# An mLSTM cell on one core: C0 and v as the stationary side of the samples' numerators, and the prompt's sums of weights first

## What is computed

```python
w = jnp.exp(dlog - m_t[..., None])
s_inter = jnp.exp(inter - m_t)
qk = jnp.einsum('bthd,bshd->bhts', qc, kc) * w
num = s_inter[..., None] * jnp.einsum('bthd,bhde->bhte', qc, cm) + jnp.einsum('bhts,bshe->bhte', qk, vc)
den = s_inter * jnp.einsum('bthd,bhd->bht', qc, nv) + jnp.sum(qk, axis=-1)
h = num / jnp.maximum(jnp.abs(den), jnp.exp(-m_t))[..., None]
...
c_new = dec[..., None, None] * cm + jnp.einsum('bshd,bshe->bhde', kw, vc)
```

## Time and profile before

| | us |
|---|---|
| median of three runs | 2201.51 |
| the profiled execution | 2201.16 |
| its span in the profile | 2199.4 |
| TensorE matmul busy | 2156.8 |
| VectorE busy | 1244.7 |
| GpSimd busy | 1203.1 |
| ScalarE busy | 423.2 |

### The profile page before, as it was taken

How to read it: one execution, slowest core, us unless ns; L and a number is a source line. 1 busy time by engine, 2 the same in 40 slices (tenths; PEclk the granted TensorE clock), 3 DMA queues, 4 the chain that set the end, 5 groups by cost and what they waited for, 6 DMA issues and landing times. The chain is left out here.

```text
span 2199.4 us, 38981 instructions
## 1 busy us (share of the span) xinstructions
PE 2156.8 (98%) x15839; PEld 2019.4 (92%) x15839; DVE 1244.7 (57%) x2095; ACT 423.2 (19%) x780; POOL 1203.1 (55%) x1228
## 2 busy tenths in 40 slices
PE   9989899999999999999999999999999999999998
PEld 9988789989999999999999995587699999999997
DVE  6888875454625344676557645772754364435263
ACT  6224541222000000121202113421422220000002
POOL 7675666526656655666657650032254365665663
PEclk9999999999999999999999999999999999999999
DMA  6224344212222222224433323552332122222221
GB/s 219 77 87 145 112 144 192 78 39 78 77 95 78 77 82 89 76 92 153 152 145 136 142 100 141 203 192 78 120 137 75 39 79 95 77 79 94 77 78 62
DMA packets 41809, 235.95 MB, mean 107 GB/s; under 512 B 4672, under 2 KB 10048, under 8 KB 16584
## 3 DMA queue, kind: packets, MB, share of 16 engines
q1 hardware_dynamic: 24512, 157.57, 20.2%
q10 hardware_dynamic: 17160, 76.38, 9.1%
HBM read 200.05 MB, written 33.89 MB: 106 GB/s over the span
## 5 line engine op out<-in xcount | busy, mean ns | idle before, releaser
L501 POOL TENSOR_TENSOR wlo<-raw,whi 128x512 fp32r<-128x512 f32 (+1 forms) x684 | 827.4, 1219 | 112.6 <-ACT whi L1253 69.9
L494 POOL TENSOR_SCALAR whi<-raw 128x512 fp32r<-128x512 f32 x512 | 365.3, 714 | 824.1 <-PE psum L596 771.3
L596 PE MATMUL psum<-xnh,whi 128*128 128x288 f32 (+1 forms) x2784 | 607.6, 296 | 13.2 <-DVEq L210 3.6
L596 PE MATMUL psum<-xnh,wlo 128*128 128x288 f32 (+1 forms) x2784 | 603.9, 295 | 0.0
L596 PE MATMUL psum<-xnl,whi 128*128 128x288 f32 (+1 forms) x2784 | 603.8, 295 | 0.0
L596 PEld LDWEIGHTS psum<-xnh,whi 128*128 128x128 f32 x2784 | 451.9, 189 | 20.4 <-issue 11.8
L596 PEld LDWEIGHTS psum<-xnh,wlo 128*128 128x128 f32 x2784 | 451.8, 189 | 0.0
L596 PEld LDWEIGHTS psum<-xnl,whi 128*128 128x128 f32 x2784 | 451.8, 189 | 0.0
L596 PE MATMUL psum<-hh,whi 128*128 128x288 f32 x992 | 212.0, 295 | 2.1 <-DVE hl L2330 2.1
L596 PE MATMUL psum<-hl,whi 128*128 128x288 f32 x992 | 211.8, 294 | 0.0
L596 PE MATMUL psum<-hh,wlo 128*128 128x288 f32 x992 | 210.7, 293 | 0.0
(11 more groups left out here) (459 smaller groups left out, 2766.1 us busy)
## 6 DMA issues: line engine op xcount, KB each, us to landing
raw<-in_w SPq DMA_DIRECT2D x145, 1024.0 KB, 4.8
C<-in_C ACTq DMA_DIRECT2D x4, 1024.0 KB, 4.8
o_cp<-mvt ACTq DMA_DIRECT2D x4, 1024.0 KB, 3.9
o_cs<-C ACTq DMA_DIRECT2D x4, 1024.0 KB, 6.5
t_xc<-xc ACTq DMA_DIRECT2D x3, 1152.0 KB, 7.3
t_z<-mv ACTq DMA_DIRECT2D x3, 1152.0 KB, 4.1
t_q<-mq ACTq DMA_DIRECT2D x3, 1152.0 KB, 4.2
t_k<-mk ACTq DMA_DIRECT2D x3, 1152.0 KB, 4.2
```

What stands on the lines that cost most here:

```text
L494: pool.tensor_scalar(whi[:, s, c], raw[:, s, c], 1.0, 1.0, ALU.mult, ALU.mult).then_inc(S("slab_hi"), 1)
L501: ins = pool.tensor_tensor(wlo[:, s, c], raw[:, s, c], whi[:, s, c].bitcast(F32), ALU.subtract)
L596: ins = pe.matmul(bank(g, 2 * m + b)[:, 0:t1 - t0], W[wi][:, kk, m0 + m, :], r[:, kk, t0:t1], start=(at_first and wi == 0 and r is rh), st ...
```

## The change

In the group `den` the order becomes: the prompt's sums of weights (four products, which need only `wt`), the sample's sums with `n0b` (after the wait for `cell_qs`), the sample's sums with `ones` (after `cell_smp`), and last, after the wait for C0 (`cell_c`), the sample's numerators. These are now made feature-major at once: for each of the four blocks of 128 features, four products with a 128x128 block of C0 as stationary side and `qs` (64 columns) moving, and one with a 64x128 block of `vt5` stationary and `wts` (64 columns) moving, all added up in the same 64 columns of bank 3. The five 512-column products, ScalarE's copy of their result, the four transposes and the two signals between them are gone. The thresholds of the two semaphores at the end of the cell are renumbered.

```diff
                 pe.wait_ge(S("cell_pt"), n + 1)
-                pe.wait_ge(S("cell_qs"), n + 1)
-                pe.wait_ge(S("cell_smp"), n + 1)
-                pe.wait_ge(S("cell_c"), 16 * (n + 1))
-                for d in range(ML_T):
-                    mm(B[2][0:TS, :], qs[:, d, :], C0[:, d, :], d == 0, False)
-                mm(B[2][0:TS, :], wts[:], vt5[:], False, True).then_inc(S("bank_filled"), 1)
                 for j in range(NTB):
                     mm(B[0][:, P * j:TP], ones[:], wt[:, blk(j):blk(j) + TP - P * j], j == 0, j == NTB - 1)
+                pe.wait_ge(S("cell_qs"), n + 1)
                 for d in range(ML_T):
                     mm(B[1][:, 0:TS], n0b[:, d, :], qs[:, d, :], d == 0, False)
+                pe.wait_ge(S("cell_smp"), n + 1)
                 mm(B[1][:, 0:TS], ones[0:TS, :], wts[:], False, True)
-                pe.wait_ge(S("bank_read"), n + 1)
+                pe.wait_ge(S("cell_c"), 16 * (n + 1))
                 for e in range(ML_T):
-                    ins = pe.transpose(B[3][:, TS * e:TS * e + TS], tm[0:TS, 1, P * e:P * e + P], ident[0:TS, 0:TS])
+                    out = B[3][:, TS * e:TS * e + TS]
+                    for d in range(ML_T):
+                        mm(out, C0[:, d, P * e:P * e + P], qs[:, d, :], d == 0, False)
+                    ins = mm(out, vt5[:, P * e:P * e + P], wts[:], False, True)
                 group_close(ins, g)
...
-            pe.wait_ge(S("bank_read"), ML_H + 1)
+            pe.wait_ge(S("bank_read"), 1)
...
-                act.wait_ge(S("bank_filled"), ML_H + 1)
+                act.wait_ge(S("bank_filled"), 1)
...
-                act.wait_ge(S("bank_filled"), n + 1)
-                act.activation(tm[0:TS, 1, 0:ML_DH], bank(GR["cell", h, "den"], 2)[0:TS, :], ACT.Copy).then_inc(S("bank_read"), 1)
```

## The result

The changed kernel takes 2215.49 us (median of six runs) against 2203.07 us of six runs of the kernel before beside it. The ratio is 1.0062, with a 95% interval of 1.0052 to 1.0072: 11 to 16 us slower, where I had forecast no difference that can be told. The profiled execution has a span of 2215.2 us against 2199.4. The page of the changed kernel, the lines that answer to the earlier trace rows, does not show why at this grain: TensorE is busy for as large a share as before.

What follows compares the result with a forecast made beforehand. TensorE, busy 98% of the span at a granted clock of nine tenths or more, bounds the kernel. Heads' 0.35 + 0 + 0.46 + 0.46 = +1.27 us on 2201.16 gave 2202.4, stated as 2202.6; range 2198.6 to 2205.0.

Steps and rivals of the forecast that it cites:

- The start of `den`: `den` no longer waits first for C0, so it opens earlier: -0.44 us in the first head, -0.22 in the others.
- The products: In `den`, 4.90 us per head removed, four blocks of 1.40 us (5.60) added; net +0.79 first head, +0.68 others.
- a sign of being wrong: The prediction called itself wrong if `den` is under 8.0 or over 10 us.
- The price of a change of shape: In `den`, a weight load switching between 128 and 64 rows costs 0.15 us more than one staying in shape.
- Rival (a): Changes of shape in `den` cost nothing: -2.6 us, 2198.6; chance 13%.
- rival (c): In `den`, each record waits for its predecessor's sum in PSUM: 0.27 us a record, +27 us, 2228; chance 6%.
- rival (b): `den` starts no earlier, since freeing the PSUM half is as late as C0: +2.3 us, 2203.5; chance 15%.
- ScalarE: Its 0.59 us copy goes, its first-head sums start some 4 us earlier; worth nothing for TensorE.
- the forecast's 1.27: Predicted net slowdown over four heads, in us: 0.35 + 0 + 0.46 + 0.46.
- The 0.49 us at `kv`: Second head's `kv` already stands 0.49 us for ScalarE's last read of `den`, so that head's +0.46 counts 0.
- Slower by over 0.2%: Whole kernel slower by more than 4.4 us, from records waiting on PSUM and a little of a no-earlier `den` start; 8%.

Runs made afterwards that it cites:

- rows_128: The changed kernel with `vt5` and `wts` filled up with rows of zeros, so `den` has no change of shape; 0.9993 of the kernel before, 1.5 us below.
- double_columns: The changed kernel with `qs` and `wts` moved twice, 128 columns, the copy into unused columns of bank 3; 1.0014 of the kernel before, 3.1 us above.
- swap_only: The kernel before with the operand swap alone, in the old order, blocks first in `den`; 1.0051 of the kernel before, 11 us above.
- cols_48: rows_128 with 48 of the 64 sample columns moved in the C0 and v products; 1.0016 of the kernel before, 3.5 us above.
- cols_32: rows_128 with 32 of the 64 sample columns moved in the C0 and v products; 1.0035 of the kernel before, 7.7 us above.
- v_pairs: The changed kernel with two blocks' C0 products, then their two v products, and again: 6 changes of shape per head, not 10; 1.0033 of the kernel before.
- run 64: Not a run or kernel: the words come from "it had run 64-column products", where TensorE executed products with 64 moving columns.
- change_again: The changed kernel itself run once more, beside cols_48 and cols_32 on the same chip; 1.0075 of the kernel before, 16.5 us above.

## Why the prediction was wrong

**The start of `den`: right in place, a bit small.** From `kT` to `den` are 2.69 us in the first head of the changed kernel, 3.32 before: -0.63, where I took -0.44 with a bound of -0.62. The bracket of the row names VectorE's signal now, as the step said it would. In the second head 1389.54 - 1387.73 = 1.81 against 2.03: -0.22, as forecast.

**The products: right at the full clock, and only there.** Block 1.40 us, `den` 9.14 us in the first head, both as computed. In the second head `den` is 11.06 us, over the 10 us that the prediction itself named as a sign of being wrong. The price of a change of shape, 0.15 us from two rows, is 0.14 by rows_128. Rival (a), that it costs nothing, is out; rival (c), that each record waits for its predecessor, is out too (0.11 a record); rival (b) is out, since `den` starts earlier in both heads above.

**ScalarE: right.** In the changed kernel its sums start at 1337.65 in the first head instead of 1342.29, and nobody gains by it.

**The failed step** is one that the prediction did not even count as a step. It read the page's clock row, nine tenths or more in every slice, as a constant of the kernel, took every duration at 2.4 GHz, and summed them for a stretch that the kernel before doesn't have: 1344.90 - 1338.02 = 6.9 us in which TensorE does nothing but 64-column products bound by their loads. That a row of nines is no proof of one level could be seen in the kernel before. Its last slice reads nine like the others, and this is the view of its last 7.5 us, in which TensorE has no work left and the granted clock is 0.50:

```profile
2191.90:2199.40 7.50, 0.00 (x0) 0.00 (x0) 2.30 (x5) 1.25 (x3) 2.29 (x3) 0.50 0.45 157
```

Rows 5 seemed to be the proof that such a run keeps its pace, but that run is half as long, and has no change of shape in it. rows_128 and double_columns show that each of the two by itself would have been harmless (a run of 64-column products without a change of shape; the ten changes of shape with 128 columns), swap_only that both together lower the clock in the old order too, and cols_48 and cols_32 that fewer columns do what the stalls do. That the stalls act by thinning the stream is argued from these, not measured. The missing term is 15.31 - 1.08 = 14.2 us for 30.7 us at half the clock, where 1.08 is the forecast's 1.27 less the first head's 0.19; half of 30.7 would be 15.3.

**Where it is paid.** Mostly not in `den`. In the first head all of it lies in `num`, dense 512-column work that had nothing to do with the change (+1.66 us); in the second `num` takes 11.54 us instead of the 8.73 that it needs, and the last two blocks 2 us more. The 0.49 us at `kv`, which was to swallow the second head's loss, is small beside that.

**The range and the chances.** The range ended at 2205.0, since its upper bound was built from terms of 0.1 us around one mechanism. Slower by over 0.2% had 8%, on a mechanism that rows of the kernel before already spoke against. A second level of the clock, at which a block takes 2.51 us instead of 1.40, was in no rival.

**Left open.** Why the change's falls are longer than those of cols_48 and cols_32 isn't settled. cols_48 was made to move about as many columns in a given time as the change, and has 17 us of falls instead of 30.7; the change's blocks also last longer, 5.6 us against 4.5. What TensorE did ahead of `den` isn't varied in any run: the same 16 transposes and a wait of 0.7 us stand there in the second to fourth head of every kernel, the kernel before too. And v_pairs shows that near the edge a single trace doesn't tell what most executions do.

## What to carry to other kernels

Turning the operands round so that fewer columns move does not make products cheaper once the weight load sets the pace (0.11 us a record with 32, 48 or 64 columns), and it takes work from the array for a stretch; before summing durations for a new stretch, ask whether the kernel has a stretch of that kind and length, and what clock was granted there. If one has to stand, keep it of one shape (with rows of zeros a block took 1.12 us instead of 1.40) or move more columns than are needed: 128 instead of 64 cost 0.10 us a block and gave the clock back. Read the granted clock by stretches of some microseconds around the edit, since a page in slices of 55 us shows nine tenths for all of this.

## What the runs showed of the hardware that I had not expected

The granted clock fell from 2.4 to 1.2 GHz while TensorE was busy for all of the 8.80 us before, with no idle time that the profile shows: it had run 64-column products, one record every 0.11 us, with stalls of 0.14 us at changes of shape among them. It rose again while dense products were running. The Trainium skill, TensorE: Matmul & The Clock Gate, Part 1, What's actually happening, gives the lower clock as the state after idle stretches of TensorE; and the same page, A second HAM failure mode, ties changes of the clock to frequent very short idle times between groups of matmuls. By the first `den` was safe, and the trace disagrees. The stalls at changes of shape could be of the second kind, but in cols_32 `den` has none of these and its clock falls, 24 us in four heads. So neither accounts for these traces. With 128 columns instead of 64 (double_columns) the clock stayed at 1.00.

A product with 64 rows among products with 128 rows costs 0.14 us at each side beyond its own loads. The Trainium skill, TensorEngine Tiling (Array Packing), Key Properties, says that a change of mode drains the engine; rows_128, where the only difference is rows of zeros, shows the price: 1.12 instead of 1.40 us a block.

Short falls of the clock also appear away from the edit, each of about 3.4 us, or twice that. They come at few places and not in every execution. In the profiles of all seven kernels that were first run after the change, and of the two with fewer columns, one lies some 10 us ahead of `den` in the first head, where the clock is 0.50 for about 3.4 us, but in neither of the first traces of before and after, nor in that of change_again. Others stand in layer 0, near 131 us in five of the twelve profiles and near 158 us in three. A single profile pair can differ by a microsecond or two for that reason alone.
